# Expert biases as pairs of 64-row products inside the sums, from a table written twice

## What is computed

```python
logits = xf @ router_w + router_b
top_vals, top_idx = lax.top_k(logits, TOP_K)           # 4 of 32
gates = softmax(top_vals)
# rows sorted by expert, in blocks of 128; for the block xb of expert e:
gu  = xb @ w_gu[e] + b_gu[e]                           # 128 x 2048
glu = minimum(gu[:, :1024], 7.0)
lin = clip(gu[:, 1024:], -7.0, 7.0)
act = glu * sigmoid(1.702 * glu) * (lin + 1.0)
y   = act @ w_dn[e] + b_dn[e]                          # 128 x 1024
# y * gate is added to the tokens' rows
```

## Time and profile before

| | |
|---|---|
| median of 3 executions | 2343.35 us (2341.95 to 2346.4) |
| the profiled execution | 2342.93 us |
| its span from the first to the last instruction | 2341.1 us |
| TensorE busy | 2165.4 us, 92% of the span |
| VectorE, ScalarE, GpSimd busy | 78%, 58%, 24% |
| mean granted TensorE clock | 0.948 of full speed |
| loop of experts | from about 825 us to about 2301 us |

### The profile page before, as it was taken

One profiled execution on the slowest core, in us unless ns is written; L12 is line 12 of the kernel. 1 busy time (PEld: TensorE's weight loads), 2 busy tenths in 40 slices (PEclk: granted clock), 3 DMA queues, 4 the chain that ended last, 5 costly groups with the idle time before them and its releaser, 6 DMA issues.

```text
span 2341.1 us, 41559 instructions
## 1 busy us (share of the span) xinstructions
PE 2165.4 (92%) x15487; PEld 1731.2 (74%) x15487; DVE 1834.0 (78%) x2152; ACT 1366.4 (58%) x1545; POOL 552.2 (24%) x434
## 2 busy tenths in 40 slices
PE   6899999867899399999999999999999999999994
PEld 5667888755678377778778778778778778778773
DVE  3699999948733777877877877877877877877885
ACT  4542223865742457667667667667667667667665
POOL 1007786764000102112112112112112112112110
PEclk8779999967999699999999999999999999999997
DMA  5011211020023279889889889889889889889896
GB/s 142 19 46 37 55 45 54 24 75 35 1 84 126 96 267 340 310 290 346 309 287 348 309 285 348 312 285 351 310 282 349 310 285 348 312 286 344 315 374 256
DMA packets 253598, 526.46 MB, mean 225 GB/s; under 512 B 33048, under 2 KB 59800, under 8 KB 253180
## 3 DMA queue, kind: packets, MB, share of 16 engines
q1 hardware_dynamic: 240268, 483.27, 57.6%
q0 software_dynamic: 13264, 42.34, 7.5%
HBM read 490.96 MB, written 35.91 MB: 225 GB/s over the span
## 4 chain that ended last, share of the span: by engine, by line
PE 70%; DMA 10%; DVE 8%; ACT 4%; issue 4%; POOL 2%; SPq 0%; DVEq 0%; ACTq 0%; POOLq 0%
PE ps L1754 13%; PE ps L1756 12%; PE ps L1755 12%; DMA e_raw<-in_w_gate_up_dram 9%; PE ps L1761 9%; PE ps L1429 5%; PE ps L1430 5%; PE ps L1431 5%; DVE e_wlo L2253 2%; PE ps L1766 1%; PE ps L1504 1%; PE ps L1634 1%; PE ps L1645 1%; PE ps L1584 1%; DVE a_s L2031 1%
## 5 line engine op out<-in xcount | busy, mean ns | idle before, releaser
L1312 ACT ACTIVATE e_whi<-e_raw 128x2048 fp32r<-128x2048 f32 x411 | 786.2, 1918 | 421.3 <-PE ps L1756 309.0
L2253 DVE TENSOR_TENSOR e_wlo<-e_raw,e_whi 128x2048 fp32r<-128x2048 f32 x410 | 926.8, 2286 | 66.3 <-ACT e_whi L1312 64.8
L1754 PE MATMUL ps<-e_whi,xh 128*128 128x512 f32 x1088 | 434.7, 400 | 0.0
L1755 PE MATMUL ps<-e_whi,xl 128*128 128x512 f32 x1088 | 424.3, 390 | 0.0
L1756 PE MATMUL ps<-e_wlo,xh 128*128 128x512 f32 x1088 | 424.1, 390 | 0.0
L941 POOL DMA_INDIRECT x_d<-ym,scur x34 | 70.6, 2078 | 871.0 <-ACT ym L1345 850.8
L1754 PEld LDWEIGHTS ps<-e_whi,xh 128*128 128x128 f32 x1088 | 204.3, 188 | 52.7 <-issue 12.9
L1756 PEld LDWEIGHTS ps<-e_wlo,xh 128*128 128x128 f32 x1088 | 204.3, 188 | 43.9
L1755 PEld LDWEIGHTS ps<-e_whi,xl 128*128 128x128 f32 x1088 | 204.5, 188 | 39.4
L1754 PE MATMUL ps<-e_whi,ath 128*128 128x512 f32 x544 | 221.7, 408 | 12.9 <-DVE atl L2281 12.9
L1756 PE MATMUL ps<-e_wlo,ath 128*128 128x512 f32 x544 | 213.3, 392 | 0.0
(11 more groups left out here) (351 smaller groups left out, 3345.1 us busy)
## 6 DMA issues: line engine op xcount, KB each, us to landing
e_raw<-in_w_gate_up_dram SPq DMA_DIRECT2D x275, 1024.0 KB, 5.2
e_raw<-in_w_down_dram SPq DMA_DIRECT2D x136, 1024.0 KB, 11.4
w_raw<-in_w_in_dram SPq DMA_DIRECT2D x20, 512.0 KB, 3.8
xt<-in_x_dram SPq DMA_DIRECT2D x8, 512.0 KB, 6.2
xr<-in_x_dram SPq DMA_DIRECT2D x8, 512.0 KB, 4.2
x_d<-x SPq DMA_DIRECT2D x8, 512.0 KB, 2.6
h_d<-h SPq DMA_DIRECT2D x8, 512.0 KB, 2.9
x<-x_d SPq DMA_DIRECT2D x8, 512.0 KB, 7.4
```

Of the source, the lines that this page charges most:

```text
L1312: nc.scalar.activation(e_whi[:, m % HRING, :], e_raw[:, m % RING, :], ACT.Copy).then_inc(s.e_hi, 1)
L1754: nc.tensor.matmul(dst, a_hi, slot_hi, start=False, stop=False, skip_group_check=True)
L1755: nc.tensor.matmul(dst, a_lo, slot_hi, start=False, stop=False, skip_group_check=True)
L2253: nc.vector.tensor_tensor(e_wlo[:, m % HRING, :], e_raw[:, m % RING, :], e_whi[:, m % HRING, :].bitcast(F32), ALU.subtract).then_inc(s.e_l ...
```

## The change

The table `bias` is written twice: rows 64 to 95 hold the high parts again, and rows 96 to 127 the rests. `rowe` has no -1 any more, so `sel` has ones in four rows, two of the upper and two of the lower half of 64. `bias_into` takes one half of 64 rows: half 0 for one bank and half 1 for another, in two instructions that follow each other. They stand inside the sums: in step 1 and step 5 ahead of the last three products (for the gate's bank 0, whose sum runs, and the up bank 1, whose sum they start), and in step 8 ahead of the second half of the products (banks 4 and 5). The sums of banks 0, 4 and 5 are now started by their first product. The products `in_groups` take all 128 rows as before, so `selo` is multiplied with a new constant `half` that is zero below row 64. Before the loop two more pairs of loads are issued, ScalarE makes one copy of 128 partitions and two of 32 instead of two of 32, GpSimd no longer clears the lower half but makes the second rests there, and some waits count anew.

```diff
+    put("half", np.tile((i < 2 * E).astype(np.float32)[:, None], (1, OVER)))
...
-    put("rowe", np.where(i < 2 * E, i % E, -1).astype(np.float32)[:, None])
+    put("rowe", (i % E).astype(np.float32)[:, None])
...
-            for h in range(2):
+            for h in range(P // E):
                 rows = slice(E * h, E * h + E)
                 sp.dma_start(braw[rows, 0:2 * D], I["b_gate_up"][0, :, :]).then_inc(s.ld_bias, 16)
                 sp.dma_start(braw[rows, 2 * D:3 * D], I["b_down"][0, :, :]).then_inc(s.ld_bias, 16)
...
-            nc.gpsimd.memset(bias[2 * E:P, :].bitcast(F32), 0.0).then_inc(s.g_bias, 1)
...
+            gp.wait_ge(s.a_bias, 1)
+            lows = slice(3 * E, 4 * E)
+            nc.gpsimd.tensor_tensor(bias[lows, :], braw[lows, :], bhi[lows, :].bitcast(F32), ALU.subtract).then_inc(s.g_bias, 1)
...
-            act.wait_ge(s.ld_bias, 80)
+            act.wait_ge(s.ld_bias, 144)
             act.wait_ge(s.g_bias, 1)
-            nc.scalar.activation(bias[0:E, :], braw[0:E, :], ACT.Copy).then_inc(s.a_bias, 1)
-            nc.scalar.activation(bhi[E:2 * E, :], braw[E:2 * E, :], ACT.Copy).then_inc(s.a_bias, 1)
+            nc.scalar.activation(bhi[:], braw[:], ACT.Copy).then_inc(s.a_bias, 1)
+            for h in range(2):
+                rows = slice(2 * E * h, 2 * E * h + E)
+                nc.scalar.activation(bias[rows, :], braw[rows, :], ACT.Copy).then_inc(s.a_bias, 1)
...
-            def three(dst, a_hi, a_lo, slot_hi, slot_lo, last):
+            def three(dst, a_hi, a_lo, slot_hi, slot_lo, last, first=False):
 
-                nc.tensor.matmul(dst, a_hi, slot_hi, start=False, stop=False, skip_group_check=True)
+                nc.tensor.matmul(dst, a_hi, slot_hi, start=first, stop=False, skip_group_check=True)
...
-            def bias_into(dst, chooser, c0):
-                nc.tensor.matmul(dst, chooser, bias[:, c0:c0 + 512], start=True, stop=False, skip_group_check=True)
+            def bias_into(dst, h, c0, first):
+
+                rows = slice(2 * E * h, 2 * E * h + 2 * E)
+                nc.tensor.matmul(dst, sel[rows, :], bias[rows, c0:c0 + 512], start=first, stop=False, skip_group_check=True)
...
-                if half == 0:
-                    pe.wait_ge(s.e_act, u.nth(8, 4 * j + (6 if g else 5)))
-                    bias_into(ps[:, g, :], sel[:], D * g + 512 * j)
+                if p % 4 == 0:
+                    pe.wait_ge(s.e_act, u.nth(8, 4 * j + 5))
                 high(u, p)
...
+                if p % 4 == 1:
+                    pe.wait_ge(s.e_act, u.nth(8, 4 * j + 6))
                 low(u, p)
                 hi_, lo_ = gu_piece(e_whi, p % HRING), gu_piece(e_wlo, p % HRING)
                 for c in range(4):
                     k = 4 * half + c
-                    m = three(ps[:, g, :], xh[:, buf, k, :], xl[:, buf, k, :], hi_[:, c, :], lo_[:, c, :], half == 1 and c == 3)
+                    if p % 4 == 1 and c == 3:
+                        for b in range(2):
+                            bias_into(ps[:, b, :], b, D * b + 512 * j, b == 1)
+                    m = three(ps[:, g, :], xh[:, buf, k, :], xl[:, buf, k, :], hi_[:, c, :], lo_[:, c, :], half == 1 and c == 3,
+                              g == 0 and k == 0)
...
                     pe.wait_ge(s.e_y, u.nth(1, 1))
-                    for b in range(2):
-                        bias_into(ps[:, 4 + b, :], sel[:], 2 * D + 512 * b)
                 high(u, p)
...
                 for c in range(2):
                     k = 2 * q + c
+                    if k == 1:
+                        for b in range(2):
+                            bias_into(ps[:, 4 + b, :], b, 2 * D + 512 * b, False)
...
-            b(nc.vector.tensor_scalar(selo[:], const("ones", c1=OVER), selcol[:, ROW_L:ROW_L + 1], None, ALU.mult))
-            dve.wait_ge(s.a_bias, 2)
+            b(nc.vector.tensor_scalar(selo[:], const("half"), selcol[:, ROW_L:ROW_L + 1], None, ALU.mult))
+            dve.wait_ge(s.a_bias, 1)
```

More of the change, by code:

```diff
@@ L897, in _ @@
             gp.wait_ge(s.p_lg, NT)
-            nc.gpsimd.memset(bias[2 * E:P, :].bitcast(F32), 0.0).then_inc(s.g_bias, 1)
             gp.wait_ge(s.v_x2, NT)
+            nc.gpsimd.memset(fresh[:], 1.0).then_inc(s.g_bias, 1)
             gp.wait_ge(s.g_bias, 1)
-            nc.gpsimd.memset(fresh[:], 1.0).then_inc(s.g_bias, 1)
+            nc.gpsimd.memset(fresh[:, :, 0:1], 0.0).then_inc(s.g_bias, 1)
             gp.wait_ge(s.g_bias, 2)
-            nc.gpsimd.memset(fresh[:, :, 0:1], 0.0).then_inc(s.g_bias, 1)
+            nc.gpsimd.tensor_tensor(earlier[:], const("before"), const("ones"), ALU.subtract).then_inc(s.g_bias, 1)
             gp.wait_ge(s.g_bias, 3)
-            nc.gpsimd.tensor_tensor(earlier[:], const("before"), const("ones"), ALU.subtract).then_inc(s.g_bias, 1)
+            nc.gpsimd.tensor_copy(every[:], const("ones")).then_inc(s.g_bias, 1)
             gp.wait_ge(s.g_bias, 4)
-            nc.gpsimd.tensor_copy(every[:], const("ones")).then_inc(s.g_bias, 1)
+            gp.wait_ge(s.a_bias, 1)
+            lows = slice(3 * E, 4 * E)
+            nc.gpsimd.tensor_tensor(bias[lows, :], braw[lows, :], bhi[lows, :].bitcast(F32), ALU.subtract).then_inc(s.g_bias, 1)
             for k in range(2):
@@ L961, in _ @@
             gp.wait_ge(s.st_yo, 16)
+            gp.wait_ge(s.g_bias, 5)
             gp.wait_ge(s.v_idx, 4)
@@ L1712, in _ @@
                     logits(t - 1)
-            pe.wait_ge(s.g_bias, 5)
+            pe.wait_ge(s.g_bias, 4)
             pe.wait_ge(s.v_dest, CHOSEN_STEPS)
@@ L1834, in dn_step @@
                     k = 2 * q + c
+                    if k == 1:
+                        for b in range(2):
+                            bias_into(ps[:, 4 + b, :], b, 2 * D + 512 * b, False)
                     for b in range(2):
                         bs = slice(512 * b, 512 * b + 512)
-                        m = three(ps[:, 4 + b, :], ath[:, k, :], atl[:, k, :], hi_[:, c, bs], lo_[:, c, bs], k == KC - 1)
+                        m = three(ps[:, 4 + b, :], ath[:, k, :], atl[:, k, :], hi_[:, c, bs], lo_[:, c, bs], k == KC - 1, k == 0)
                     if q == 1 and c == 0:
@@ L1865, in _ @@
             pe.wait_ge(s.v_be, BE_STEPS)
-            pe.wait_ge(s.a_bias, 2)
+            pe.wait_ge(s.a_bias, 3)
             pe.wait_ge(s.g_bias, 5)
@@ L2102, in _ @@
             d.done()
-            dve.wait_ge(s.g_bias, 3)
+            dve.wait_ge(s.g_bias, 2)
             d(nc.vector.tensor_tensor_scan(upto[:].rearrange("p e t -> p (e t)"), fresh[:].rearrange("p e t -> p (e t)"),
@@ L2191, in _ @@
             d(nc.vector.tensor_copy(rowf[:], rowi[:]))
-            dve.wait_ge(s.ld_bias, 80)
+            dve.wait_ge(s.ld_bias, 144)
             d.done(1)
@@ L2303, in choose @@
                 if both:
-                    c = nc.vector.tensor_scalar(selo[:], const("ones", c1=OVER), selcol[:, bass.ds(col, 1)], None, ALU.mult)
+                    c = nc.vector.tensor_scalar(selo[:], const("half"), selcol[:, bass.ds(col, 1)], None, ALU.mult)
                 c.then_inc(s.e_sel, 1)
```

## The result

The changed kernel takes 2359.11 us (median of 4 executions, 2356.96 to 2360.95) against 2344.81 us before (2341.95 to 2346.4): a ratio of 1.0062 with a 95% interval of 1.0045 to 1.0079. It is slower by about 14.3 us; 8.3 were forecast. (A fourth execution has moved the median of the kernel before from 2343.35 to 2344.81.) The profiled execution has a span of 2355.2 us, 14.1 more than before.

What follows compares the result with a forecast made beforehand. The prediction took the loop to run at TensorE's pace, with transfers also near their limit in S. Pairs +16.3 less 8.0 from waits gave +8.3, thus 2351.7 us, range 2344 to 2363.

Steps and rivals of the forecast that it cites:

- The direction: Whole kernel: slower than before, given a chance of 0.77.
- The forecast of 0.61 us for a pair: TensorE in the loop: 0.24 plus 0.37 for two shape changes, against 0.454; +16.3 us over 102 pairs.
- What the waits give back: TensorE's 18 waits for `atl` in units S and X shrink as it arrives later: -8.0 us.
- the steady wait: Step 10 of each steady unit S: the 0.55 us wait for `atl` falls by 0.44, not below 0.11.
- The rival in which the transfers move along: Loop: transfers shift with TensorE, nothing is given back; +16.3, 2359.7 us, chance 0.14.
- other edits: Waits and stage before the loop: ScalarE's copies +2.8 us, GpSimd's subtraction up to 7.3 if it held VectorE; none charged.
- the likeliest case's own range: Whole kernel, with a pair at 0.61 us: 2348 to 2356 us.
- The stated range: Whole kernel: 2344 to 2363 us, covering the likeliest case, the second, and an unforeseen few us before the loop.
- signs of being wrong: Profile: 0.23 to a pair and 0.24 after, `atl` waits still 0.55, new step 5 wait, or longer stage before the loop.
- The longer loads and ScalarE's third copy: Before the loop: three copies of 2.76 us instead of two, +2.8 us ahead of a 14.5 us wait; not charged.
- The moved waits: Up bank wait moves to steps 1 and 5, step 4's 2.7 us between; priced at nothing unless VectorE was later.
- A pass: One pass of the loop: grows by six pairs' 0.98 less 0.44, some 0.5 us.

Runs made afterwards that it cites:

- Full_inside: Kernel before with its full-array products, the six moved to the change's places inside the sums; 2344.51 us, ratio 0.9995.
- joined_pairs: Table_by_vector with the pair of down moved to step 5, directly behind that of gate and up; 2346.18 us, ratio 1.0006 to the kernel before.
- No_bias: Kernel before without the 204 full-array products of the bias table; 2337.27 us, ratio 0.9972.
- Table_by_vector: Changed kernel with GpSimd's subtraction given to VectorE, ScalarE writing high parts afterwards; 2353.74 us, ratio 1.0041 to the kernel before.
- gpsimd_alone: Kernel before plus one GpSimd subtraction of 32 partitions by 3072 into rows nobody reads; 2353.07 us, ratio 1.0029.
- pairs_at_groups: Table_by_vector with L's pairs only at steps 0 and 4, full products in S; 2365.25 us, ratio 1.0080 to the kernel before.

## Why the prediction came out as it did

**The direction and the mechanism were right.** The halves run side by side (two products within 0.01 us, 0.23 for a second pair), and each pair pays two changes of shape. The forecast of 0.61 us for a pair was 0.63: the sum had +0.16 a pair, and the three gaps of all 102 pairs (medians 0.319, 0.431 and 0.338 us, together 1.088, against four of 0.227) give +0.18, 18.4 us instead of 16.3; a change of shape is nearer to 0.20 us than to the 0.19 of the forecast. Full_inside shows it is the form and not the place, joined_pairs that it is the change of shape and not the pair.

**What the waits give back was right**: 8.0 forecast, 7.7 measured, and the steady wait falls to 0.10 us where the sum had 0.11. The loop's 10.6 are 18.4 less 7.7, but that they meet so well is in part luck: unit X's clock gave back 1.7 us more, of which the prediction has no word, and small amounts spread over the units, some 1.6 us in all, went the other way; no run tells what they are. No_bias shows the mechanism from the other side: a unit S is held at 37.3 to 37.5 us. The rival in which the transfers move along is out: it wanted +16.3 in the loop and waits that stay at 0.55, and its total, 2359.7, is near the measured one by accident only, since 3.6 us of that come from before the loop.

**The step that failed** stands under other edits: "If it held up VectorE, which makes the chain at that time, it could cost up to 7.3 us; no row shows two engines so, and I take nothing." It did, with 4.4 us on one instruction. The error was in the word "nothing": I had looked at what GpSimd's instruction hides behind (34.4 us of its own idle time) and took its cover for the answer, while the question was which other engine runs during it and whether they share something. Table_by_vector takes it away, gpsimd_alone makes it by itself. The measured 2359.1 lies outside the likeliest case's own range, 2348 to 2356. Of the 7.4 us over the forecast of 2351.7, 3.6 come from before the loop, 2.3 from the loop and 1.5 from the median of the kernel before. The stated range held the result because it left room for a few unforeseen us before the loop, not because the prediction knew of them; a stage before the loop that is longer by some us was one of its own signs of being wrong.

**The other terms.** The longer loads and ScalarE's third copy cost nothing, as priced: the changed kernel's stage before the loop loses less than the 4.4 us of the held instruction, and table_by_vector, which has the loads and the copy of 128 partitions but makes the other two copies later, starts its loop no later than the kernel before (at 827.77 instead of 829.43). The moved waits cost nothing at steps 1 and 5, with step 4 as their cover; pairs_at_groups took the cover away and paid 22.6 us, which is what that sentence of the prediction warned of. A pass was forecast to grow by 0.5 us (where six pairs' 0.98 should read 0.96); it grows by 0.72.

## What to carry to other kernels

Packing two half-height products side by side halves their stream but in this kernel costs a fixed price on the way in and out, so it pays for runs of them or where the array changes its shape anyway, and loses for a single pair between full products. Before a piece of preparation goes to GpSimd, look at what VectorE does during that time: an instruction off the critical path can hold one that is on it. And where one kind of unit is bound by its transfers, count gains and losses on TensorE only in the other kind.

## What the runs showed of the hardware

- A change of the array's shape costs 0.19 to 0.20 us, about 0.09 ahead of it and 0.10 to 0.11 behind, for row halves (joined_pairs) as for column groups; a product of 64 by 128 by 512 beside its twin costs 0.23 us for both.
- GpSimd's subtraction of 32 by 3072 (6.65 us) held a VectorE `tensor_scalar` of 32 elements for 4.4 us and a scan with two inputs in SBUF for 6.4, and let MAX8 (0.20 us) and MATCH_REPLACE8 (0.18 us) pass.
- Where TensorE's waits had grown from 0.55 to some 1.85 us (no_bias), the granted clock fell to its lower level for 3.4 us behind half of them, 1.6 us each time; behind the waits of 0.55 us it never did. The first unit X shows it the other way round, with a wait of 2.1 us before and 1.4 after. A gain on TensorE that turns into waiting can so lose much of what it gains.
